# Last attention: ScalarE instead of VectorE copies the output blocks out of PSUM, and the norm's low part moves to the end of VectorE's step

## The reference

```
z = einsum('bqhd,bkhd->bhqk', q, k) * scale          # 16 heads, 64 wide
log_beta = log_sigmoid(z)
log_keep = where(valid, log_beta - z, 0)             # valid: key strictly before the query
after = cumsum(log_keep, axis=3, reverse=True) - log_keep
w = where(valid, exp(log_beta + after), 0)
y_sb = rms_norm(einsum('bhqk,bkhd->bqhd', w, v), sb_norm_g)
mix = concatenate([y_ssd, y_sb]) @ w_out             # y_ssd: gated state-space output, rms-normed
```

## Time and profile before

| | us |
|---|---|
| median of 3 runs | 1615.33 |
| lowest, highest | 1614.38, 1616.31 |
| the profiled execution | 1612.91 |
| its span | 1611.1 |
| last attention, in the span | about 850 to 1138 |

### The profile page before, as it was taken

One profiled execution on the slowest core, in us unless ns is written; L12 is line 12 of the kernel. 1 busy time (PEld: TensorE's weight loads), 2 busy tenths in 40 slices (PEclk: granted clock), 3 DMA queues, 4 the chain that ended last, 5 costly groups with the idle time before them and its releaser, 6 DMA issues.

```text
span 1611.1 us, 28791 instructions
## 1 busy us (share of the span) xinstructions
PE 1546.4 (96%) x10686; PEld 1352.3 (84%) x10686; DVE 1024.8 (64%) x1602; ACT 507.3 (31%) x1047; POOL 885.3 (55%) x830
## 2 busy tenths in 40 slices
PE   5999999999999999999988999998999999999998
PEld 4888877897888888999987888887998998988886
DVE  4499847469828876865767878875336666565002
ACT  4311012131137763333345555554214110111001
POOL 1455431567684408663428744344572777777981
PEclk9999999999999999999999999999999999999999
DMA  9437421323210002232111111112131333333331
GB/s 320 125 118 210 156 72 53 92 66 92 79 52 2 23 6 79 79 92 65 41 40 50 43 53 53 39 44 62 53 92 40 91 91 91 91 94 111 121 118 52
DMA packets 188971, 131.11 MB, mean 81 GB/s; under 512 B 5279, under 2 KB 171711, under 8 KB 188751
## 3 DMA queue, kind: packets, MB, share of 16 engines
q1 hardware_dynamic: 188878, 129.82, 26.5%
HBM read 127.71 MB, written 2.10 MB: 81 GB/s over the span
## 4 chain that ended last, share of the span: by engine, by line
PE 87%; DVE 7%; ACT 3%; issue 2%; DMA 1%; SPq 0%; DVEq 0%; ACTq 0%
PE ps L2316 20%; PE ps L2317 19%; PE ps L2319 19%; PE ps L3048 3%; PE ps L3047 3%; PE ps L3046 3%; PE ps L2640 2%; PE ps L2664 2%; PE ps L2961 2%; DVE sb_sum L2147 2%; PE ps L2627 1%; DMA ada_first<-in_ada_w 1%; DVE op_lo L1538 1%; PE ps L2869 1%; PE ps L2937 1%
## 5 line engine op out<-in xcount | busy, mean ns | idle before, releaser
L773 POOL TENSOR_SCALAR w_hi<-raw 128x512 fp32r<-128x512 f32 x322 | 244.4, 759 | 600.3 <-PE ps L2319 229.2
L775 POOL TENSOR_TENSOR w_lo<-raw,w_hi 128x512 fp32r<-128x512 f32 x322 | 462.2, 1435 | 26.8
L2316 PE MATMUL ps<-xn_hi,w_hi 128*128 128x264 f32 (+1 forms) x800 | 234.2, 313 | 8.5 <-ACT q_even L1285 3.3
L2316 PE MATMUL ps<-op_hi,w_hi 128*128 128x512 f32 x608 | 215.6, 355 | 1.6 <-DVE op_lo L1538 1.4
L2317 PE MATMUL ps<-xn_lo,w_hi 128*128 128x264 f32 (+1 forms) x800 | 212.7, 286 | 0.0
L2317 PE MATMUL ps<-op_lo,w_hi 128*128 128x512 f32 x608 | 204.9, 354 | 0.0
L2319 PE MATMUL ps<-op_hi,w_lo 128*128 128x512 f32 x608 | 177.9, 352 | 0.0
L2316 PEld LDWEIGHTS ps<-xn_hi,w_hi 128*128 128x128 f32 x800 | 152.1, 190 | 21.9 <-issue 13.5
L2316 PE MATMUL ps<-u_hi,w_hi 128*128 128x258 f32 (+1 forms) x528 | 162.1, 321 | 0.9 <-DVE u_lo L2208 0.4
L2319 PE MATMUL ps<-xn_hi,w_lo 128*128 128x264 f32 (+1 forms) x800 | 162.9, 285 | 0.0
L2317 PE MATMUL ps<-u_lo,w_hi 128*128 128x258 f32 (+1 forms) x528 | 162.0, 320 | 0.0
(11 more groups left out here) (458 smaller groups left out, 3211.2 us busy)
## 6 DMA issues: line engine op xcount, KB each, us to landing
raw<-in_w_in SPq DMA_DIRECT2D x45, 512.0 KB, 3.6
raw<-in_w_up SPq DMA_DIRECT2D x44, 512.0 KB, 3.7
ada_ring<-in_ada_w SPq DMA_DIRECT2D x14, 1024.0 KB, 5.3
raw<-in_w_down SPq DMA_DIRECT2D x22, 512.0 KB, 3.2
raw<-in_w_in_ab SPq DMA_DIRECT2D x20, 512.0 KB, 5.5
raw<-in_w_in_c SPq DMA_DIRECT2D x20, 512.0 KB, 3.7
ada_first<-in_ada_w SPq DMA_DIRECT2D x4, 2048.0 KB, 16.4
raw<-in_w_out SPq DMA_DIRECT2D x16, 512.0 KB, 3.8
```

The lines of the kernel that those rows point to most:

```text
L773: steps(nc.gpsimd.tensor_scalar(hi, r, 1.0, 0.0, ALU.mult, ALU.add))
L775: nc.gpsimd.tensor_tensor(lo, r, hi.bitcast(F32), ALU.subtract)\
L2316: mm(o[:, 512 * b:512 * b + n], w_h[:, k, :], hi[:, k0 + k, c0:c0 + n], start=a, stop=False)
```

## The change

In ScalarE's step the output copies of u-3 stand right behind the copies of the transposed weights of u-2, ahead of everything else, as `nc.scalar.copy`; in VectorE's step they are gone. The low part of the norm goes from the front of VectorE's step to its end, behind `sb_start` of u+1. The semaphores (`sb_o` before the copy, `sb_y` after it) are the same.

```diff
 # ScalarE, sb_iteration, step u
                         ins.then_inc(s["sb_wc"], 1)
+                    for w in sb_out_now(u - SB_SKEW) if sb_live(i, u - SB_SKEW) else ():
+                        m, par, blk, nq, q0, nk, buf = sb_unit(w)
+                        n = P if blk else META
+                        h = sb_out(w)
+                        act.wait_ge(s["sb_o"], 2 * NT * i + h + 1)
+                        o = sb_bank(w)[:, 0:n].unsqueeze(1)
+                        nc.scalar.copy(ysb[:, bass.ds(2 * i + m, 1), q0:q0 + n], o).then_inc(s["sb_y"], 1)
                     if last and u - 1 in MIX_TAIL:
 # VectorE, sb_iteration, step u
                 for u in range(sb_steps(last)):
-                    if u - 1 in sb_norm(i):
-                        ... low part of the norm, L2125 ...
-                    for w in sb_out_now(u - SB_SKEW) if sb_live(i, u - SB_SKEW) else ():
-                        m, par, blk, nq, q0, nk, buf = sb_unit(w)
-                        n = P if blk else META
-                        h = sb_out(w)
-                        dve.wait_ge(s["sb_o"], 2 * NT * i + h + 1)
-                        o = sb_bank(w)[:, 0:n].unsqueeze(1)
-                        nc.vector.tensor_copy(ysb[:, bass.ds(2 * i + m, 1), q0:q0 + n], o).then_inc(s["sb_y"], 1)
                     if sb_live(i, u - 1):
                         ... scan and subtraction of u-1 ...
                     if sb_scored(u + 1, last):
                         sb_start(i, u + 1)
+                    if u - 1 in sb_norm(i):
+                        ... low part of the norm, as above ...
```

More of the change, by code:

```diff
@@ L2162, in sb_iteration @@
                         sb_start(i, u + 1)
+                    if u - 1 in sb_norm(i):
+                        j = sb_norm(i)[u - 1]
+                        if not isinstance(i, int) or j:
+                            dve.wait_ge(s["op_hi"], OP_DONE["pre"] + sb_norm_chunk(i, j) + 1)
+                        else:
+                            dve.wait_ge(s["op_hi"], OP_DONE["pre"] + 1)
+                            dve.wait_ge(s["gated"], KC)
+                        nc.vector.scalar_tensor_tensor(ys_lo[:, bass.ds(sb_norm_chunk(i, j), 1), :],
+                                                       zs[:, bass.ds(sb_norm_chunk(i, j), 1), PAD:TP],
+                                                       cols[:, 0, bass.ds(sb_norm_chunk(i, j) + COL["ssd_norm"], 1)],
+                                                       ys_hi[:, bass.ds(sb_norm_chunk(i, j), 1), :].bitcast(F32),
+                                                       ALU.mult, ALU.subtract)\
+                          .then_inc(s["op_ready"], 1)
             steps(nc.vector.memset(v_sb[:, :, 0, :], 0.0))
```

## The result

| | median us | runs |
|---|---|---|
| before | 1615.27 | 8 (1613.39 to 1617.85) |
| changed | 1622.74 | 8 (1619.24 to 1624.96) |

The ratio is 1.0045, with a 95% interval of 1.0034 to 1.0057: 7.5 us more (5.5 to 9.2). The forecast was 1621.8 us, in a range of 1615 to 1626.

A forecast was written before the change was run, and what follows sets the result against it. The prediction took TensorE, 96% busy, as the bound and priced edits as its gaps. Losses of 13.3 us less gains of 6.8 gave +6.5: 1619.4 from the profiled 1612.91, plus 2.4 to the median, 1621.8 us, range 1615 to 1626.

The forecast's parts named there:

- scores of units 6 and 15: Steps 5 and 14: TensorE's scores wait for ScalarE's late output copies, 0.97 us four times and 1.13 three times.
- scores of units 8 and 17: Steps 7 and 16: scores wait for ScalarE's 128x384 output copy, 0.48 us seven times, 3.4 us lost.
- low part ahead of units 7 and 16: Steps 7 and 16: the norm's low part now precedes VectorE's scan, costing 0.3 us four times, 1.2 us.
- ends of pairs: units 8, 9, 12 together: Transposes at nine-unit pair ends: gains of 1.8 and 2.5 us; scores of unit 12 lose 1.5 us.
- the chain take, Exp and Ln, transposed weights, Exp: ScalarE at pair ends, from taking v to the first unit's Exp: 1.90 us, limiting gains to 0.35 of 0.90.
- both chains: Units 6 and 15: ScalarE's copy and TensorE's scores both follow TensorE's last slab chunk, so slack elsewhere cannot shorten the wait.
- Its cost there goes too, 1.24 each, 2.5 us: Two pairs with the norm in step 10: moving the low part behind unit 9's scan removes its cost.
- part 1: Copy leaves VectorE: the scan at a pair's last unit starts about 2.6 us sooner; gains sum to 6.8 us.
- Unit 12's waits: Step 11: scores wait for ScalarE's output copy, some 0.3 us three times, 0.6 in the last pair, 1.5 us.
- (a): Rival: ScalarE reaches the copies in time, leaving only the gains, -6.8 us, 1608.5 us; chance 0.11.
- (b): Rival: a draw; waits at units 6 and 15 come, 7.2 us, others hidden by slack, 1615.7 us; chance 0.17.
- (c): Rival: larger loss from ScalarE delays at each new wait and low part meeting GpSimd, about 1627 us; chance 0.12.

The follow-up runs named there:

- e3: Changed kernel with ScalarE's output copies of u-2 at the end of step u, ahead of Exp and Ln of u+1: 1609.99 us, ratio 0.9970 to the kernel before.
- e4: Changed kernel with ScalarE's output copies of u-3 moved ahead of the transposed weights of u-2: 1616.04 us, ratio 1.0003 to the kernel before.
- e6: Kernel before, copies kept on VectorE, those of units 6 and 15 behind a later subtraction, low part behind the subtraction: 1610.29 us, ratio 0.9967.
- e1: Changed kernel with the norm's low part back at the front of VectorE's step, output copies still on ScalarE: 1620.75 us, ratio 1.0038 to the kernel before.
- e5: e3 with the norm's low part on VectorE right behind the subtraction of u-1: 1607.99 us, ratio 0.9956 to the kernel before.
- e7: e5 with Exp and Ln of u+1 ahead of ScalarE's take of v in steps 0 and 9: 1605.15 us, ratio 0.9935 to the kernel before.
- e2: Kernel before with only the norm's low part moved to the end of VectorE's step, output copies staying on VectorE: 1615.10 us, ratio 0.9998.

## Why the prediction was right

The time lies 0.9 us from the forecast and inside its range, and the waits are those that it named. The steps of the sum against the stage, in microseconds, worked out from the starts of the scores in both traces:

| step | forecast | trace |
|---|---|---|
| scores of units 6 and 15, seven waits | +7.2 | +7.4 |
| scores of units 8 and 17, seven waits | +3.4 | +4.1 |
| low part ahead of units 7 and 16 | +1.2 | +1.2 |
| ends of pairs: units 8, 9, 12 together | -2.8 | -2.3 |
| two single waits, 909.97 and 931.99 | -1.2 | -1.0 |
| last unit | -1.3 | -1.5 |
| sum | +6.5 | +7.9 |

The first row is +6.12 us in the intervals to these units, +0.6 in the ones behind them, where the scores run 0.1 us longer after a wait, and 0.7 that the single wait lying in the same interval gave back. The second is +3.56, +0.25 behind them, and 0.3 of the single wait at 909.97. (Four times 0.97 is 3.9 and not the 3.8 of the forecast's sum, which changes nothing.)

**Right, and shown by experiments.** That the place in ScalarE's queue decides (e3 and e4, with nothing else changed), that the price of the copy itself does not matter (e3, e6), that the low part costs 0.3 us at four places (e1, e5), and that the chain take, Exp and Ln, transposed weights, Exp is late next (e7). That both chains start from the same event, so that slack elsewhere hides nothing, fits the traces but had no experiment of its own: the intervals to units 6 and 15 grew by nearly one size, 0.88 to 1.09 us, but for the one with a single wait beside it.

**Right in sum, wrong in the parts.** "Its cost there goes too, 1.24 each, 2.5 us" was put down to the low part's new place in step 10. e1 has the old place and the same gain: the removed copy had made it. The low part's move brings the change nothing there, gives it 0.7 us at a single wait and costs it 1.2 us; alone it is no change (e2). "In its other steps TensorE has cover of over 1 us" was wrong for step 10: e3 against e5 shows 0.45 us in each loop iteration. And part 1 counted on a scan that starts 2.6 us sooner; it did not count on one that is also 0.5 to 0.8 us shorter, which e2 shows to be enough to close the first gap. The gain came out right since the chain behind it sets the second gap, as the forecast has it.

**Small errors of size.** Six of the seven waits at units 8 and 17 held the scores up by 0.41 to 0.48 us, as forecast or a little less; the intervals behind them grew by about 0.1 us, which the forecast did not price. The seventh was 0.93 instead of 0.48: the scan of unit 14 ran from 907.40 for 2.06 us beside GpSimd's squares (1.85 in the kernel before, 0.98 in the other pairs of the loop), so the mask addition of unit 16 came late. Unit 12's waits came to 1.25 us instead of 1.5 (its four intervals against those of e3). Unit 10, whose bank is also held by an output of the step just before, has no term in the forecast, and none was needed: 0.00 to 0.02 us in the three pairs without the low part there. The forecast's "about 20 waits and 13 us" counted the three old waits and all of unit 12's; the rows have 15 and 9.5, and some more that the trace gives as "issue".

**The rivals.** (a) would have needed the copies in time. e3 is that case, 4 us below the kernel before, less than (a)'s 6.8 us since it keeps the low part's cost. e5 has that cost no more, and without its clock in the first pair its stage would be 6.8 us shorter than before. (b) fell with the 3.56 us at units 8 and 17. (c) did not come: the intervals to units 6 and 15 grew by what the forecast had (0.88 to 1.09 us against 0.97 and 1.13), and the low part ran into GpSimd only in step 10.

The rule of the Trainium skill's "Perfetto Trace Analysis" (optimizing Scalar/DVE operations), that work may go to ScalarE where VectorE is saturated, did not decide here: VectorE is busy for 62% to 64%, and e6 gains about as much as e3 without moving anything to ScalarE. The rule on the shared port of the Trainium skill's "SBUF — State Buffer" (SBUF: two separate sides) agrees with the rows shown under e2, and with the low part itself, which took 1.07 and 1.08 us in step 10 of the changed kernel's loop iterations and 0.76 elsewhere. It was held up there as the prediction feared; only the gain that this was to eat did not hang on its place.

## What to carry to other kernels

When an operation that frees a buffer moves to another engine, its own duration is the least of it: look at what stands ahead of it in that engine's queue, and at how soon the producer comes back for the buffer. Put it right where its input becomes ready, and work that nobody waits for behind it. And when an engine idles long in front of a wait, first try to move that one wait behind work that is ready, on the same engine; here two of ten copies per iteration carried nearly all of the gain. Look too at what runs beside an instruction that is moved: the same scan took 1.25 or 2.39 us by whether it started before or behind GpSimd's instruction.

## What the runs showed of the hardware

A scan of 528 columns with two inputs in SBUF took 1.25 us where it started 0.13 us before GpSimd's split, which then took 2.20 us, and 2.39 us where it started 0.01 us behind it, with the split at 1.29 (e2). In the first pair TensorE's granted clock was 0.50 up to 858 us or up to 861 us, after the same waits of TensorE; the longer stretch cost e5 1.2 us. A TensorE wait costs more than its bracket: 0.75 us idle made the scores start 0.88 us later and last 0.94 instead of 0.83 us. A copy of 128x128 from PSUM is about as long on ScalarE (0.25 us) as on VectorE (0.29), and the next instruction on ScalarE starts 0.1 us before it ends.
